# Retention moved between the attention's score tiles in a two-layer hybrid encoder step

## What is computed

```python
[A | B | C inputs] = rms_norm(x) @ w_in[l]              # 2816 columns
A: band attention, 4 heads of 64; streams also read 256 cached keys and values
B: retention, 4 heads, keys of 64, values of 128:
   att = (q @ k.T) * decay;  o = att @ v + (q * q_dec) @ state
   state = state * s_dec + (k * k_dec).T @ v
   o = silu(gate) * group_norm(o) * ret_gn_g
C: GLU, causal depthwise convolution of width 31, layer norm, silu
x = x + concat(A, B, C) @ w_out[l]
x = x + cross_attention(rms_norm(x), mk, mv)            # mk = mem @ wx_k, mv = mem @ wx_v
x = x + ffn(rms_norm(x))                                # layer 0 dense, layer 1 eight experts
```

## Time and profile before

| | |
|---|---|
| median of 3 runs | 1863.4 us (1862.84 to 1864.01) |
| profiled execution | 1861.05 us, its span 1859.2 us |
| mean granted clock of TensorE | 0.961 |
| busy: TensorE / VectorE / ScalarE / GpSimd | 91% / 52% / 40% / 7% |

### The profile page before, as it was taken

One profiled execution on the slowest core, in us unless ns is written; L12 is line 12 of the kernel. 1 busy time (PEld: TensorE's weight loads), 2 busy tenths in 40 slices (PEclk: granted clock), 3 DMA queues, 4 the chain that ended last, 5 costly groups with the idle time before them and its releaser, 6 DMA issues.

```text
span 1859.2 us, 21936 instructions
## 1 busy us (share of the span) xinstructions
PE 1696.7 (91%) x7878; PEld 1254.9 (67%) x7878; DVE 958.8 (52%) x1427; ACT 736.5 (40%) x1044; POOL 124.3 (7%) x243
## 2 busy tenths in 40 slices
PE   6998799988898998999987998788999999999996
PEld 3454555756677788744546466577888888888885
DVE  1621333334322334218025233357888898888987
ACT  2114112422422323211131224334776777777775
POOL 2230110000000000030302000000000000000000
PEclk9999899999898999999988999987999999999998
DMA  7535334262532333242432432744998988988983
GB/s 258 167 92 174 114 105 158 80 249 95 178 101 80 136 113 124 90 119 89 150 127 94 158 136 91 272 154 163 313 316 290 325 297 298 321 306 293 320 303 140
DMA packets 176142, 343.47 MB, mean 185 GB/s; under 512 B 6939, under 2 KB 48173, under 8 KB 175809
## 3 DMA queue, kind: packets, MB, share of 16 engines
q1 hardware_dynamic: 163808, 319.31, 50.3%
q0 software_dynamic: 3920, 12.58, 2.2%
q10 hardware_dynamic: 8352, 10.75, 1.6%
HBM read 332.58 MB, written 11.90 MB: 185 GB/s over the span
## 4 chain that ended last, share of the span: by engine, by line
PE 83%; ACT 6%; DVE 5%; issue 3%; DMA 1%; POOL 0%; ACTq 0%; DVEq 0%; SPq 0%; POOLq 0%
PE bank L1082 21%; PE bank L1121 15%; PE bank L1122 14%; PE bank L1123 14%; PE bank L1069 4%; PE bank L1193 3%; PE bank L1099 2%; PE bank L1573 2%; ACT arena L1650 2%; DVE arena_parts L875 1%; ACT arena_parts L871 1%; DMA ring<-in_w_in 1%; PE bank L1199 1%; PE bank L1522 1%; PE bank L1551 1%
## 5 line engine op out<-in xcount | busy, mean ns | idle before, releaser
L1121 PE MATMUL bank<-arena_parts,features_parts 128*128 128x512 f32 (+1 forms) x960 | 373.3, 389 | 23.3 <-DVE arena_parts L746 9.5
L1122 PE MATMUL bank<-arena_parts,features_parts 128*128 128x512 f32 (+1 forms) x960 | 368.3, 384 | 0.0
L1123 PE MATMUL bank<-arena_parts 128*128 128x512 f32 (+1 forms) x832 | 325.3, 391 | 0.0
L875 DVE TENSOR_TENSOR arena_parts<-ring,arena_parts 128x1024 fp32r<-128x1024 f32 (+1 forms) x246 | 279.8, 1155 | 38.3 <-ACT arena_parts L871 33.4
L1082 PE MATMUL bank<-ring,features_T 128*128 128x512 f32 (+1 forms) x672 | 272.7, 568 | 2.8 <-ACT features_T L1650 2.8
L871 ACT ACTIVATE arena_parts<-ring 128x1024 fp32r<-128x1024 f32 (+1 forms) x246 | 243.5, 1007 | 67.4 <-PE bank L1123 64.1
L1082 PEld LDWEIGHTS bank<-ring,features_T 128*128 128x128 f32 x672 | 128.3, 192 | 143.2 <-issue 137.1
L1121 PEld LDWEIGHTS bank<-arena_parts,features_parts 128*128 128x128 f32 x960 | 183.3, 191 | 56.0 <-issue 16.5
L1650 ACT ACTIVATE arena<-bank 128x512 f32<-128x512 f32 (+3 forms) x160 | 85.0, 567 | 340.6 <-PE bank L1082 202.8
L1122 PEld LDWEIGHTS bank<-arena_parts,features_parts 128*128 128x128 f32 x960 | 183.3, 191 | 31.0
L1123 PEld LDWEIGHTS bank<-arena_parts 128*128 128x128 f32 x832 | 159.4, 192 | 32.2
(11 more groups left out here) (280 smaller groups left out, 1807.1 us busy)
## 6 DMA issues: line engine op xcount, KB each, us to landing
ring<-in_moe_w_up SPq DMA_DIRECT2D x41, 1024.0 KB, 6.7
ring<-in_moe_w_down SPq DMA_DIRECT2D x30, 1024.0 KB, 5.1
ring<-in_moe_w_gate SPq DMA_DIRECT2D x22, 1024.0 KB, 6.9
ring<-in_w_in SPq DMA_DIRECT2D x20, 1024.0 KB, 5.3
mem_kv<-in_moe_w_gate SPq DMA_DIRECT2D x20, 1024.0 KB, 5.3
ring<-in_cache_mem_k SPq DMA_DIRECT2D x16, 1024.0 KB, 6.8
ring<-in_cache_mem_v SPq DMA_DIRECT2D x16, 1024.0 KB, 7.0
ring<-in_moe_w_gate SPq DMA_DIRECT2D x20, 768.0 KB, 6.1
```

The source lines that it names most:

```text
L875: nc.vector.tensor_tensor(self.part(p, 1), self.raw(p), self.part(p, 0).bitcast(F32), ALU.subtract).then_inc(self.split, 1)
L1121: nc.tensor.matmul(out, left[0], right[0], start=start, stop=False)
L1122: nc.tensor.matmul(out, left[0], right[1], start=False, stop=False)
L1123: return nc.tensor.matmul(out, left[1], right[0], start=False, stop=stop)
```

## The change

`psum_jobs` lists the same order. Memory and shapes:

```diff
-        m.at = at0
-        attT = cut(m.take(BH * TOK), h=BH)
-        attS = cut(m.take(BH * P), h=BH)
-        q0 = cut(m.take(BH * 512), h=BH)
-        ks = m.take(BH * 512).rearrange("p (h n d) -> p h n d", h=BH, n=NS)
+        attT = cut(fT_[:, 2 * TOK:6 * TOK], h=BH)
+        attS = cut(fT_[:, 6 * TOK:6 * TOK + BH * P], h=BH)
...
+        q0 = up_[:, 0:BH * P].rearrange("p (h j c) -> p h j c", h=BH, j=4)
+        ks = us_[:, 0:BH * P].rearrange("p (h i d) -> p h i d", h=BH, i=2)
```

attT and attS lie in the features that the projection's left side takes later, q0 and ks in the convolution's input. TensorE, beside the moves:

```diff
+                    for new in range(2):
                         for n2 in range(2):
                             for k in range(2):
...
+                                if new:
+                                    ins = nc.tensor.matmul(b[g:g + 32, 256:384], qblk[:, k, s_, :],
+                                                           qkA[:, 2 + k, 256:384], start=True, stop=True)
+                                else:
+                                    nc.tensor.matmul(b[g:g + 32, 0:256], qblk[:, k, s_, :], ktA[:, s_ % 4, k, :],
+                                                     start=True, stop=True)
...
+                for h in range(BH):
+                    nc.tensor.matmul(b[:, h * P:(h + 1) * P], attS[:, h, :], v_(2, h), start=True, stop=False)
+                    for j in range(4):
+                        ins = nc.tensor.matmul(b[32 * j:32 * j + 32, h * P:(h + 1) * P], q0[:, h, j, :], s0[:, j, h, :],
+                                               start=False, stop=True)
+                end(ins, "oB", l, 2)
...
+                    for t in range(3):
+                        for n2 in range(2):
+                            for k in range(2):
...
+                                ins = nc.tensor.matmul(b[row:row + 32, r * P:(r + 1) * P], pTS[:, r, t, row:row + 32],
+                                                       right, start=(t == 0), stop=(t == 2))
...
+                b = [begin("nsS", l, j) for j in range(4)]
                 for h in range(BH):
+                    for j in range(4):
+                        ins = nc.tensor.matmul(b[j][:, h * P:(h + 1) * P], ks[32 * j:32 * j + 32, h, :, :],
+                                               proj[32 * j:32 * j + 32, 2, VB + h * P:VB + (h + 1) * P],
+                                               start=True, stop=True)
...
-                wait_emptied(pe, "ocT", l, 1)
+                def turned(k, t):
+                    if t == 0:
+                        wait_emptied(pe, "obT", l, min(max(k - 2, 0), BH - 1))
```

The last one makes the projection wait for the copies of obT one 128-row block at a time. ScalarE: the store of mk is issued before the copies of qkA, qkB and mkT; all ktA copies and that of nsP come before all exponentials; the copy of oA comes after the second of pTS; and the Silu moves ahead of the second half of mv:

```diff
                 copy(svals, bank[BANK[("oS", l)][0]][:, :], "oS", l)
+                act.wait_ge(s_lnr, 2 * l + 2)
+                A(proj[:, :, CA:CA + CC], proj[:, :, CA:CA + CC], ACT.Silu).then_inc(s_oc, 1)
+                memory_rows("mv", mv, 1)
```

VectorE: the decays stand between the streams' scores, the statistics of the convolution and the (now 512 columns wide) q0 before the softmax scaling, the rest of the convolution's layer norm after it, then:

```diff
+                group_stats(0)
+                group_stats(1)
+                group_scale(0)
+                group_scale(1)
+                group_stats(2)
+                group_scale(2)
+                for j in range(4):
+                    wait_filled(dve, "nsS", l, j)
+                    for h in range(BH):
+                        st.did(V.scalar_tensor_tensor(
+                            s0[:, j, h, :], s0[:, j, h, :], GAMMA[h] ** TS,
+                            bank[BANK[("nsS", l, j)][0]][:, h * P:(h + 1) * P], ALU.mult, ALU.add),
+                            emptied["v"] if h == BH - 1 else None)
```

More of the change, by code:

```diff
@@ L179, in psum_jobs @@
         for j in range(4):
+            one(("mkT", l, j), "a")
+        for j in range(4):
             one(("sA", l, j), "v")
[L181 removed]
+        for n in range(4):
             one(("ktA", l, n), "a")
[L183 to L184 removed]
+        for r in range(4):
+            if r < 2:
+                one(("aB", l, 2 * r), "v")
+                one(("aB", l, 2 * r + 1), "v")
+            elif r == 2:
+                for j in range(2):
+                    one(("aS", l, j), "v")
+            else:
+                one(("nsP", l), "a")
+            one(("sS", l, r), "v")
+            if r < 2:
+                one(("ktA", l, 2 * r + 4), "a")
+                one(("ktA", l, 2 * r + 5), "a")
+        for t in range(NT):
+            one(("yc", l, t), "v")
+        for t in range(2):
+            one(("oB", l, t), "v")
         memory_values(l, 0)
@@ L187, in psum_jobs @@
             one(("pTA", l, h), "a")
-        one(("oA", l), "a")
         for r in range(4):
+            if r == 2:
+                one(("oA", l), "a")
             one(("pTS", l, r), "a")
+        one(("oB", l, 2), "v")
         one(("oS", l), "a")
         for h in range(BH):
-            one(("aB", l, h), "v")
+            one(("nsS", l, h), "v")
+        memory_values(l, 1)
         one(("oST", l), "a")
[L195 to L204, removed]
+        for b in range(2):
+            one(("ocT", l, b), "a")
         for b in range(BH):
             one(("obT", l, b), "a")
-        for b in range(2):
-            one(("ocT", l, b), "a")
         product(("out", l), 2, NT, "v")
@@ L1334, in _ @@
                     end(ins, "qkB", l, t)
+                wait_emptied(pe, "mk", l, 1, 1)
+                for j in range(4):
+                    b = begin("mkT", l, j)
+                    for k in range(2):
+                        for t in range(2):
+                            ins = turn(b[:, k * 256 + t * P:k * 256 + (t + 1) * P],
+                                       mk[:, t, (2 * j + k) * P:(2 * j + k + 1) * P])
+                    end(ins, "mkT", l, j)
                 wait_emptied(pe, "qkA", l, 2)
@@ L1346, in _ @@
                     end(ins, "sA", l, j)
-                pe.wait_ge(s_blk, l + 1)
[L1349 to L1359, removed]
-                        r = n // 2
-                        wait_emptied(pe, "ktA", l, n)
-                        b = begin("sS", l, r)
+                past_keys = [None]
@@ new lines, in turn_past @@
+                def turn_past(r):
+                    for n in (2 * r, 2 * r + 1):
+                        if n % 4 == 0:
+                            past_keys[0] = slab("cache_attn_k").rearrange("p (j d) -> p j d", j=8)
+                        b = begin("ktA", l, n)
+                        for k in range(2):
+                            for t in range(2):
+                                ins = turn(b[:, k * 256 + t * P:k * 256 + (t + 1) * P],
+                                           past_keys[0][:, 2 * (n % 4) + t, k * P:(k + 1) * P])
+                        end(ins, "ktA", l, n)
@@ new lines, in prompt_decays @@
+                def prompt_decays(h):
+                    lo = 64 * (h % 2)
+                    b = begin("aB", l, h)
+                    nc.tensor.matmul(b[:, 0:256], qkB[lo:lo + 64, 2 + h // 2, 0:P], qkB[lo:lo + 64, h // 2, 0:256],
+                                     start=True, stop=True)
+                    end(nc.tensor.matmul(b[:, 256:384], qkB[lo:lo + 64, 2 + h // 2, P:2 * P],
+                                         qkB[lo:lo + 64, h // 2, P:2 * P], start=True, stop=True), "aB", l, h)
```

379 lines of the change are left out of this document (180 added, 199 removed).

## The result

| | before | after |
|---|---|---|
| median of 4 runs | 1863.7 us (1862.84 to 1864.87) | 1808.33 us (1800.47 to 1809.37) |
| profiled execution | 1861.05 us | 1808.6 us |
| ratio, 95% interval | | 0.9693 (0.9666 to 0.9721) |

A forecast was written before the change was run, and what follows sets the result against it. PE bounds the kernel, each wait paid as idle time and again as half clock. Per layer -21.5 - 6.6 - 0.9 - 5.1 + 3.0 = -31.1, two layers -62.2, so 1801 us from the 1863.4 median; range 1790 to 1826.

The forecast's parts named there:

- Idle time removed: PE's idle time between memory-key product and output projection goes through reordering: -21.5 us per layer.
- new waits: PE waits for banks DVE empties late, for obT copies and for the key store: +3.0 us per layer.
- the late end: Key store lands after 8.6 us, not 4.3; DVE's first score drain starts at 174.6, not 170.3; costs about 2 us.
- Half clock removed: PE work at 0.50 and 0.90 clock behind the long waits in the stretch returns to full clock: -6.6 us per layer.
- The projection's clock: First 17.4 us of the output projection lose 1.74 us at 0.90 clock; half taken as gain, -0.9 per layer.
- Packing: Retention's small matmuls oB2, nsS and oS packed or reordered across the array: 2.0, 2.1 and 1.0 us, -5.1 per layer.
- q0 held by POOL: DVE's q0 products, beside POOL's convolution rstd, may be held: ends 1.76 us and the earlier 6.26 us.
- my bad end: POOL's decayed keys and gains beside DVE's score work could make DVE later by their 5.5 us.
- Banks bind: Rival: q0 stays held, the key store lands late and PE stands at pTS0; 1827 us, chance 0.12.
- Slabs bind: Rival: PE runs into its weights' DMA and the time stays at 1863 us; chance 0.03.
- The long hold at pTS0: Rival: DVE far later than PE at pTS0, with half clock behind; at 25 us later, 1869 us; chance 0.05.
- Two layers: -62.2: Sum of -31.1 us per layer, taken off the profiled execution's 1861.05 us to give 1798.9.

The follow-up runs named there:

- e3_free: Changed kernel with the softmax weights' turned copies laid over the memory keys' columns, so DVE's first drain need not wait for the key store: 1799.68 us, ratio 0.9669.
- e5_before: The kernel before, unaltered, run and profiled a second time: 1859.77 us, ratio 0.9991 against the kernel before.
- e11_before_shifted: The kernel before with 24 unused constant columns, moving every buffer behind them up by 96 bytes: 1869.47 us, ratio 1.0039.
- e4_early: Changed kernel with the first memory-value product put back ahead of the prompt's scores: 1822.32 us, ratio 0.9797 against the kernel before.
- e2_pad: Changed kernel with 24 unused constant columns, so that buffers behind lie where they lay in the kernel before: 1800.38 us, ratio 0.9665.
- e7: Changed kernel with e3_free's layout and 8 unused constant columns, buffers 64 bytes below the place before: 1796.17 us, ratio 0.9649.
- e8: Changed kernel with e3_free's layout and 16 unused constant columns, buffers 32 bytes below the place before: 1798.79 us, ratio 0.966.
- e6_free_pad24: Changed kernel with e3_free's layout and 24 unused constant columns, buffers at the place before: 1794.92 us, ratio 0.9632.

## Why the prediction was right, and where it was not

*Idle time removed, new waits: right in sum, but by luck.* Forecast -21.5 and +3.0 per layer, measured 21.5 to 2.9. The places differ, and two errors cancel. The largest wait is not at pTS but at aB0, 1.5 us, behind the key store, which landed after 8.1 us, near the late end (8.6) and not the early one (4.3). The sum counted DVE from 171, the early end, and named about 2 us for the late end, with DVE's drain at 174.6; it started at 178.80, as the issue was at 170.66 and not at 166.0. But the whole stretch had moved by 4.6 us, so against the key product's end the issue was as forecast. At pTS1, where I had DVE and PE meet, PE waits 0.4 us instead of 2. e3_free shows the store's part alone (1.82 and 1.35).

*Half clock removed: right for the trace that it was read from.* PE's busy time fell by 13.45 us. The packed products account for 1.6 (oB2 at full clock), 1.9 (oS) and 2.7 (nsS), 6.2 together; the rest, about 7, is the clock, against 6.6 forecast. Every window is at 1.00. But three of the six layers of this order that were traced lost 2 to 3 us less to the half clock (e5_before, e11_before_shifted); from those traces the same term would have been about 4 to 5. *The projection's clock* gave its full 1.7 us (43.16 to 41.44), at the good end where I took 0.9.

*Packing: mis-sized, 6.2 instead of 5.1.* oB2 takes 2.9 us, not 2.4, and gave 1.6 instead of 2.0. oS gave 1.9 where I took 1.0, all that its bound allowed, and nsS 2.7 where I took 2.1, near its good end of 2.9. The view by line of the packed oS and nsS in the kernel after:

```profile
L1492 PEld LDWEIGHTS bank<-ring,arena x64: 110/110/110, 213.8 to 216.1; 128*32 128x32 f32 x64
```

```profile
L1500 PEld LDWEIGHTS bank<-arena x32: 181/187/187, 216.6 to 217.4; 32*128 32x128 f32 x32
```

With 32 more from the arena alone, 96 weight loads of 0.110 us are 10.6 us and ran within 2.7, so on the average four were under way at once; with the order by column group, the 4.6 of before came down to that. The rule that I weighed against this term, in the Trainium skill ("TensorE: Matmul & The Clock Gate", Part 3), lets weight loads overlap running matmuls only where the row group differs. All of these use the same 128 rows and differ in their columns alone, so the trace disagrees with it again, more plainly than the kernel before did. The Trainium skill ("TensorEngine Tiling (Array Packing)", Tiling Modes, Key Properties) says that tiles can load weights and multiply in parallel, and the trace agrees: four column tiles, four loads at once.

*q0 held by POOL: it did not happen.* The timeline of DVE and that of POOL in the kernel after:

```profile
191.81 0.48 DVE L2271 MEMSET arena<- 128x512 f32 x1
192.33 1.98 DVE L2277 TENSOR_TENSOR arena<-arena,consts 64x64 f32<-64x64 f32 x8
```

```profile
192.04 0.57 POOL L2569 TENSOR_TENSOR lnr<-lnr,consts 128x1 f32<-128x1 f32 x1
```

Eight products in 1.98 us from first to last, 0.25 from one to the next, with POOL's roots beside them from 191.72 to 194.5: near the forecast's 1.76, and far from the 6.26 of before. The Trainium skill ("GPSIMD Engine Reference", 1. Specifications) has DVE operations with two SBUF inputs contend with GpSimd, as q0's are. Here POOL's operations are of one column per row and hold nothing that can be seen; it was the large gate products that held them before. By the same section of the Trainium skill the score drains, which take one input from PSUM, escape. e3_free, where they run beside POOL's decayed keys and gains, has the four at 2.15 us against 1.95: 0.05 us each at most, so the 5.5 us of my bad end were far off.

*The rivals.* Banks bind (1827): no; the waits at the turns of pTA and pTS come to 0.4 us. Slabs bind: no DMA wait of PE in the stretch, though the share rose from 0.35 to 0.50. The long hold at pTS0: no. e4_early shows what it would look like, 4.8 us of wait and a clock of 0.60, when the product that covers it is taken away.

*The step that failed* is the one that was hardly written: "Two layers: -62.2", taken off the whole time of the profiled execution. It takes all other stages as unchanged. The two layers gave 67.6 us, 5.4 more than forecast, and 15.2 were lost elsewhere; that the two partly cancel brought the time nearer to the forecast. The expert loop gave 5.0 back through the place of its buffers (shown by e2_pad, e7, e8 and e11_before_shifted). The start took 4.6 and the dense part and the routing 5.7 in that execution; the last two did not come back in repeats, and the start is open. That the parts add up where the place is right can be seen in e6_free_pad24: key product to projection takes 63.3 us in layer 0 (169.92 to 233.25) and 63.7 in layer 1 (908.27 to 971.97), so 33.9 + 33.4 + 3.4 = 70.7 less 4.5 for the key product's later end and 1.3 for the loop is 64.9. Its profiled execution was 66.1 under that of the kernel before (1861.05 less 1794.92).

## What to carry to other kernels

Sum the idle time of the bounding engine and the half clock behind each long wait together: both go when independent work is put in between, and one long product as cover can be worth more than faster small ones. Read the half clock from more than one execution: here it came out 2 to 3 us apart per layer behind the same waits. When a change resizes a constant or a buffer, compare the addresses of all that lies behind it and pad back to the old place before judging the change by less than half a per cent. A store whose source is soon overwritten belongs where the next writer is late; give the early writer other columns.

## What the hardware showed that I had not expected

The same products, in the same order and at the same work, ran at two speeds by the place of their buffers modulo 64 bytes. With the buffers behind the constants 0 or 64 bytes below the old place, the loop took 584.6 to 586.0 us in six traces; 32 or 96 bytes below or 96 above, 588.4 to 590.5 in seven. No trace lies between. The medians of whole runs that differ in this alone are 2.6 to 6.9 us apart (e7 and e8, e11 and its kernel before). In the first group the 352 down products have a median of 389 to 392 ns, in the second one of 396 to 399.

The traces point at one operand. The experts' gate and up products take their left side from the features, which did not move; the down products take it from the arena, which did. Both take their right side from the split weights, which kept their place. Groups in the loop, of the kernel before and of e8_free_pad16 (32 bytes below): busy us and mean ns of one.

```profile
L1121 PE MATMUL bank<-arena_parts,features_parts 128*128 128x512 f32 x320 | 128.7, 402 | 1.9 <-DVE counts L2391 1.9
...
L1121 PE MATMUL bank<-arena_parts 128*128 128x512 f32 x220 | 86.5, 393 | 0.0
```

```profile
L1131 PE MATMUL bank<-arena_parts,features_parts 128*128 128x512 f32 x320 | 128.7, 402 | 1.9 <-DVE counts L2435 1.9
...
L1131 PE MATMUL bank<-arena_parts 128*128 128x512 f32 x220 | 87.7, 399 | 0.0
```

The first group is the same, the second slower. So it seems to be the left side's place that counts; a run that moves it alone was not made, and why 64 bytes stays open.

A record of a product over 32 columns of the array is as long as one over 128 (medians of 0.285 us at L1477 and 0.275 at L1475). What packing gains is seen in the distance of the starts alone: 96 records in 2.7 us.
